# Router logits with the padded weights as loaded operand in four column groups, and token places by 5 products in place of 14, in a two-layer hybrid trunk

## The reference

```python
logits = (t @ router).astype(F32)          # (512, 1024) @ (1024, 8)
top_v, top_i = lax.top_k(logits, TOP_K)    # TOP_K = 2
gates = jax.nn.softmax(top_v, axis=-1)
order = jnp.argsort(e_flat)                # tokens sorted by expert
counts = jnp.bincount(e_flat, length=N_EXPERTS)
out = swiglu(t[tok], w_gate[e], w_up[e], w_down[e])   # per block of one expert
```

## Time and profile before

| what | value |
|---|---|
| median of 3 runs | 2400.32 us (2399.8 to 2401.42) |
| the profiled execution | 2397.78 us |
| its span, first to last instruction | 2395.7 us |
| mean granted clock of TensorE | 0.980 |
| TensorE busy | 2268.1 us (95%) |
| VectorE, ScalarE, GpSimd busy | 1167.0, 942.6, 119.1 us |
| experts stage, from the first expert weight's issue (1166.33 us) | 1229 us of the span |

### The profile page before, as it was taken

One profiled execution on the slowest core, in us unless ns is written; L12 is line 12 of the kernel. 1 busy time (PEld: TensorE's weight loads), 2 busy tenths in 40 slices (PEclk: granted clock), 3 DMA queues, 4 the chain that ended last, 5 costly groups with the idle time before them and its releaser, 6 DMA issues.

```text
span 2395.7 us, 37781 instructions
## 1 busy us (share of the span) xinstructions
PE 2268.1 (95%) x15401; PEld 1932.3 (81%) x15401; DVE 1167.0 (49%) x1563; ACT 942.6 (39%) x1176; POOL 119.1 (5%) x177
## 2 busy tenths in 40 slices
PE   7988999999999888989899999999999998999995
PEld 6864988888878777649687777877779998999994
DVE  3267533323254678473588888888883000001001
ACT  4247432222242444373367677676772000000001
POOL 6101000000000000000000001010100000000000
PEclk9999999999999999999899999999999999999997
DMA  6320223242222000111699999999998768768663
GB/s 196 111 83 6 87 90 106 88 128 97 93 81 79 2 3 3 37 36 41 232 365 345 376 343 368 355 365 349 370 338 292 258 216 271 257 226 281 229 226 106
DMA packets 262117, 451.16 MB, mean 188 GB/s; under 512 B 8360, under 2 KB 148495, under 8 KB 261855
## 3 DMA queue, kind: packets, MB, share of 16 engines
q1 hardware_dynamic: 257216, 435.73, 52.4%
q0 software_dynamic: 4576, 13.41, 2.3%
q10 hardware_dynamic: 190, 0.05, 0.0%
HBM read 436.63 MB, written 12.52 MB: 187 GB/s over the span
## 4 chain that ended last, share of the span: by engine, by line
PE 86%; DVE 6%; ACT 4%; issue 2%; DMA 1%; ACTq 0%; DVEq 0%; POOLq 0%; SPq 0%; POOL 0%
PE bank L704 83%; PE bank L707 3%; DVE arena L2108 1%; DVE w_low L2108 1%; DVE slot L2108 1%; ACT w_high L2026 1%; ACT arena L1636 0%; ACT arena L1737 0%; ACT arena L1645 0%; DMA xs<-sum_rows_d 0%; DMA vec_rows<-in_b_norm_w_dram 0%; DMA sum_rows_d<-arena,idx_now 0%; ACT arena L1613 0%; ACT w_high L1581 0%; DVE arena L2855 0%
## 5 line engine op out<-in xcount | busy, mean ns | idle before, releaser
L2108 DVE TENSOR_TENSOR w_low<-slot,w_high 128x2048 fp32r<-128x2048 f32 x172 | 393.6, 2292 | 325.1 <-ACT w_high L1581 257.9
L704 PE MATMUL bank<-arena 128*128 128x144 f32 (+6 forms) x2672 | 344.6, 298 | 6.1 <-DVE small L2267 2.5
L704 PEld LDWEIGHTS bank<-arena 128*128 128x128 f32 (+4 forms) x2672 | 311.7, 182 | 21.7 <-issue 10.8
L704 PE MATMUL bank<-arena,slot 128*128 128x144 f32 (+4 forms) x2368 | 312.3, 301 | 10.8 <-issue 5.9
L2108 DVE TENSOR_TENSOR arena<-arena,bank 128x512 f32<-128x512 f32 (+2 forms) x99 | 58.7, 593 | 529.9 <-PE bank L704 529.9
L704 PEld LDWEIGHTS bank<-arena,slot 128*128 128x128 f32 (+2 forms) x2368 | 288.7, 184 | 30.4 <-issue 23.4
L2108 DVE TENSOR_TENSOR w_low<-arena,w_high 128x2048 fp32r<-128x2048 f32 x105 | 240.1, 2290 | 25.9 <-ACT w_high L2026 25.1
L2026 ACT ACTIVATE w_high<-slot 128x2048 fp32r<-128x2048 f32 x108 | 206.3, 1915 | 71.0 <-PE bank L704 39.3
L704 PE MATMUL bank<-w_high,xg_high 128*128 128x512 f32 x560 | 227.3, 406 | 6.3 <-DVE w_low L2108 4.2
L2026 ACT ACTIVATE w_high<-arena 128x2048 fp32r<-128x2048 f32 x105 | 201.2, 1921 | 62.3 <-PE bank L704 62.3
L704 PE MATMUL bank<-h_ffn,w_high 128*128 128x512 f32 (+1 forms) x736 | 222.7, 385 | 0.8 <-DVE w_low L2108 0.8
(11 more groups left out here) (367 smaller groups left out, 3265.5 us busy)
## 6 DMA issues: line engine op xcount, KB each, us to landing
slot<-in_moe_w_up_dram SPq DMA_DIRECT2D x86, 1024.0 KB, 6.5
arena<-in_moe_w_gate_dram SPq DMA_DIRECT2D x78, 1024.0 KB, 6.9
arena<-in_moe_w_down_dram SPq DMA_DIRECT2D x64, 1024.0 KB, 6.6
slot<-in_moe_w_down_dram SPq DMA_DIRECT2D x48, 1024.0 KB, 6.3
slot<-in_moe_w_gate_dram SPq DMA_DIRECT2D x34, 1024.0 KB, 5.2
arena<-in_moe_w_up_dram SPq DMA_DIRECT2D x26, 1024.0 KB, 5.9
slot<-in_e_w_in_dram SPq DMA_DIRECT2D x12, 1024.0 KB, 5.4
slot<-in_ff_w_gate_dram SPq DMA_DIRECT2D x11, 1024.0 KB, 5.1
```

What stands on the lines that cost most here:

```text
L704: return pe.matmul(o, lhsT, rhs, start=start, stop=True, skip_group_check=True)
L2108: return dve.tensor_tensor(o, a, b, op)
```

## The change

The operands of the logit products change places. `w_router` is padded to 32 columns with zeros and becomes the loaded operand, 128 tokens of `hT[3]` are streamed. The eight products of a token tile go to the four groups of 32 output rows in turn (k and k + 4 to the same group), so a bank then holds four partial sums of 8 rows each, by expert and token. VectorE copies this bank to `logit_parts`. One product per tile, with `logit_parts` loaded and the 128x8 matrix `group_sum` streamed, adds the four groups and turns the result back into tokens by experts. `group_sum` is built once by GpSimd from `ident`. The places take one product of 32 columns with `before` for all tiles, and one with `ones` for each of the four tiles, which adds that tile's counts to all later column groups at once.

```diff
--- before.py
+++ after.py
@@ -269,7 +269,8 @@
         vc = sb("vc", [P, 95])
         w_dt = sb("w_dt", [P, KT, HEADS])
         w_dt_high, w_dt_low = sb("w_dt_high", [P, KT, HEADS], F32R), sb("w_dt_low", [P, KT, HEADS], F32R)
-        w_router = sb("w_router", [P, KT, N_EXPERTS])
+        w_router = sb("w_router", [P, KT, 32])
+        group_sum = sb("group_sum", [P, N_EXPERTS])
         lora = sb("lora", [P, 2, C_WIDTH])
         small = sb("small", [P, 256])
         small_i = sb("small_i", [P, 16], I32)
@@ -410,6 +411,7 @@
         assert M0 + 1200 + SLOT <= S0 and len(raw_slots) == RAW
         xg_high, xg_low = rounded("xg_high", arena_at + 4 * S0, KT, P), rounded("xg_low", arena_at + 4 * (S0 + 1024), KT, P)
         hid_tok = region(S0 + 2048, 4 * P)
+        logit_parts = region(S0 + 2048, NT, P)
         hid_high = rounded("hid_high", arena_at + 4 * (S0 + 2560), 2, 2, P)
         hid_low = rounded("hid_low", arena_at + 4 * (S0 + 3072), 2, 2, P)
         h_mix = [rounded(f"h_mix{i}", arena_at + 4 * at, KT, SEQ) for i, at in enumerate((4096, 0))]
@@ -565,7 +567,8 @@
                                pattern=[[-1, P]], channel_multiplier=1).then_inc(sem("ident_ready"), 1)
             for k in range(KT):
                 pool.dma_start(w_dt[:, k, :], e_w_in[0, k * P:(k + 1) * P, DT_COL:DT_COL + HEADS]).then_inc(sem("w_dt_loaded"), 16)
-            pool.dma_start(w_router[:, :, :], moe_router[0].rearrange("(k p) e -> p k e", p=P)).then_inc(sem("router_loaded"), 16)
+            link(pool.memset(w_router[:, :, :], 0.0))
+            pool.dma_start(w_router[:, :, 0:N_EXPERTS], moe_router[0].rearrange("(k p) e -> p k e", p=P)).then_inc(sem("router_loaded"), 16)
             pool.dma_start(small[0:HEADS, 0:1], b_dt_bias[0].rearrange("(h a) -> h a", a=1)).then_inc(sem("small_loaded"), 16)
             pool.dma_start(small[0:HEADS, 1:2], b_a_log[0].rearrange("(h a) -> h a", a=1)).then_inc(sem("small_loaded"), 16)
             for r in range(2):
@@ -588,6 +591,9 @@
             pool.wait_ge(sem("bias_loaded"), 16 * HEADS)
             link(pool.memset(bias_w[CHUNK:P, :, SEQ - CHUNK:], -MASKED))
 
+            link(pool.tensor_tensor(group_sum[:, :], ident[:, 0:N_EXPERTS], ident[:, 32:32 + N_EXPERTS], ALU.add))
+            for g in (2, 3):
+                link(pool.tensor_tensor(group_sum[:, :], group_sum[:, :], ident[:, 32 * g:32 * g + N_EXPERTS], ALU.add))
             link(pool.memset(ones[:, :], 1.0))
             link(pool.memset(before[:, :], 1.0))
             select(before[:, :], ALU.is_gt, 0.0, 0, [[1, P]], -1)
@@ -1363,22 +1369,39 @@
 
             if upto >= 6:
                 pe.wait_ge(sem("router_loaded"), 16)
-                b, former = tile("logit_ready", 1)
+                def logits_by_group(t):
+                    b, former = tile("parts_ready", t + 1)
+                    pe.wait_ge(*former)
+                    for k in range(KT):
+                        if k % 4 == 0:
+                            pe.wait_ge(sem("hT_ready"), 24 + 2 * t + k // 4 + 1)
+                        g = slice(32 * (k % 4), 32 * (k % 4) + 32)
+                        m = mm(b[g, 0:P], w_router[:, k, :], hT[3][:, k, P * t:P * (t + 1)], k < 4)
+                    m.then_inc(sem("parts_full"), 1)
+
+                def logits_by_token(t):
+                    pe.wait_ge(sem("parts_ready"), t + 1)
+                    return mm(logits[:, 8 * t:8 * t + 8], logit_parts[:, t, :], group_sum[:, :], t == 0)
+
+                for t in (0, 1):
+                    logits_by_group(t)
+                logits, former = tile("logit_ready", 1)
                 pe.wait_ge(*former)
-                for t in range(NT):
-                    if t == 2:
-                        turn(3)
-                    pe.wait_ge(sem("hT_ready"), 24 + 2 * t + 2)
-                    for k in range(KT):
-                        m = mm(b[:, 8 * t:8 * t + 8], hT[3][:, k, P * t:P * (t + 1)], w_router[:, k, :], t == 0 and k == 0)
-                m.then_inc(sem("logit_full"), 1)
+                logits_by_token(0)
+                logits_by_group(2)
+                turn(3)
+                for t in (1, 2):
+                    logits_by_token(t)
+                logits_by_group(3)
+                logits_by_token(3).then_inc(sem("logit_full"), 1)
 
                 pe.wait_ge(sem("sel_ready"), 1)
                 b, former = tile("place_ready", 1)
                 pe.wait_ge(*former)
-                for t in range(NT + 1):
-                    for s in range(min(t + 1, NT)):
-                        m = mm(b[:, 8 * t:8 * t + 8], (before if s == t else ones)[:, :], sel[:, s, :], t == 0)
+                mm(b[:, 0:8 * NT], before[:, :], sel.rearrange("p t e -> p (t e)"), True)
+                for s in range(NT):
+                    later = b[:, 8 * s + 8:8 * NT + 8].rearrange("p (t e) -> p t e", e=N_EXPERTS)
+                    m = mm(later, ones[:, :], sel[:, s:s + 1, :].to_broadcast([P, NT - s, N_EXPERTS]), False)
                 m.then_inc(sem("place_full"), 1)
                 pe.wait_ge(sem("place_ready"), 1)
                 for i in range(WARM_UP):
@@ -2627,7 +2650,14 @@
 
 
             if upto >= 6:
+                def logits_taken(t):
+                    dve.wait_ge(sem("parts_full"), t + 1)
+                    dve.tensor_copy(logit_parts[:, t, :], bank["parts_ready", t + 1][:, 0:P]).then_inc(sem("parts_ready"), 1)
+
+                for t in (0, 1, 2):
+                    logits_taken(t)
                 turned(3, 3)
+                logits_taken(3)
                 L, E2 = NT * N_EXPERTS, [P, NT, N_EXPERTS, N_EXPERTS]
                 dve.wait_ge(sem("logit_full"), 1)
                 dve.tensor_copy(logit, bank["logit_ready", 1][:, 0:L].rearrange("p (t e) -> p t e", e=N_EXPERTS)).then_inc(sem("logit_ready"), 1)
```

## The result

The changed kernel takes 2378.25 us, median of 4 runs (2376.1 to 2379.18), beside 2400.06 us (2397.12 to 2401.42, 4 runs) for the kernel before. The ratio is 0.9912, 95% interval 0.9896 to 0.9927. The profiled execution took 2377.97 us, its span 2375.9, 19.8 us less than before.

What follows compares the result with a forecast made beforehand. TensorE, busy 95% of the span, was taken as the bound, with no other work covering these products. Logits 4.35 plus places 3.85 gave 8.2 us off the median 2400.3: 2392.1 us, with an 8-in-10 range of 2389.0 to 2396.5.

Steps and rivals of the forecast that it cites:

- What is hidden: Set-up: GpSimd's memset and three additions, at most 3.6 us, lie under over 40 us of cover; padding adds no transfer.
- Step 1: Logits: tiles 0 and 1 start at 1130.76 as before and end at about 1132.0.
- Step 2: Logits: VectorE is late; its 0.28 us bank copies start after `turned(3, 2)`, costing TensorE 0.3 us wait plus 0.35 us product.
- Steps 3 to 5: Logits: tile 2, `turn(3)`, then tile 3's second half at the low clock; VectorE copies the logits 4.35 us earlier.
- The mark "16 records in 0.5 to 0.6 us": Expected sign in the logits: 128x32 loads in fours, with each token tile's 16 records in that time.
- The mark of 6.5 us to the copy: Expected sign: VectorE copies the logits 6.5 us after the first logit product instead of 11.0.
- The Trainium skill's rule: Logits: loads run under a product only in another row group; 1.0 us a tile, total gain about 7.2 instead of 8.2.
- 1.7 us either way: Gathering `first_rows`: its low-clock stretch may shift, costing or saving 1.7 us, the largest term of the range.
- Two groups at a time: Rival for the logits: only two column groups overlap, eight rounds per tile; gain 7.4, 2392.9 us, chance 8%.
- no overlap at all: Rival for the logits: column groups do not run side by side; gain 1.4, 2398.9 us, chance 6%.
- Records run singly: Rival for the logits: each load and product runs to its end, 0.4 us a record; 2414 us, chance 3%.
- The low clock through all of `first_rows`: Rival for the gathering: 64 records take 15.4 us in place of 9.78; gain 2.6, 2397.7 us, chance 5%.

Runs made afterwards that it cites:

- a1_shift800: Kernel before plus an unused array of 800 bytes per partition behind `w_router`, no instruction changed: 2387.65 us, ratio 0.996.
- a2_after_plus32: Changed kernel plus 32 unused bytes per partition right ahead of the arena: 2389.65 us, ratio 0.9967 to the kernel before.
- a3_arena32: Kernel before plus 32 unused bytes right ahead of the arena alone: 2387.5 us, ratio 0.996.
- b2_logits_only: Changed kernel with the old 14 place products and 32 unused bytes ahead of the arena: 2398.99 us, ratio 1.0008 to the kernel before.
- k1_xg128: Changed kernel with the experts' loaded buffers 128 bytes further within the arena: 2375.07 us, ratio 0.9902 to the kernel before.
- h1_slots64: Changed kernel plus 64 unused bytes ahead of the weight slots, moving slots and arena alike: 2376.41 us, ratio 0.9908.
- h2_both64: Changed kernel plus 64 unused bytes ahead of the weight slots and 64 more ahead of the arena: 2387.0 us, ratio 0.9958.
- h4_both32: Changed kernel plus 32 unused bytes ahead of the weight slots, moving slots and arena alike: 2375.49 us, ratio 0.9907.

## Why the prediction was wrong

The mechanism it priced was right, and its sum was right for the stage. The failed step is in "What is hidden": it takes GpSimd's instructions as the only effect of the set-up ("The padding adds no transfer"), and so puts the new addresses at nothing without a reason. The padding and `group_sum` move every array declared after them by 768 + 32 = 800 bytes. That is worth 10.4 us by `a1_shift800` and 11 to 14 us by `a2_after_plus32`, more than the whole sum. By the rule of distances the 768 bytes, three times 256, change nothing: the 32 bytes of `group_sum` do, and `a3_arena32` has the same gain from 32 bytes alone (0.996).

- **Logits.** 4.35 us forecast, 4.7 measured, within the bounds of 3.5 and 5.2. Step 1 was 1.2 us for tiles 0 and 1 and took 1.08. Step 2, a copy at 0.28 us, was 0.28 to 0.29, and VectorE was the late one. Steps 3 to 5 kept the order given. The mark "16 records in 0.5 to 0.6 us" held for tiles 0 and 1 (1.08 us for 32) and was just missed by tile 2 (0.65). The mark of 6.5 us to the copy came out at 6.3. One small step was off: the second half of tile 3 was to run at the low clock, and the timeline's windows show 1.00 up to 1128.20.

```profile
1122.24:1128.20 5.96, 4.34 (x80) 3.28 (x79) 3.77 (x10) 2.83 (x5) 0.00 (x0) 1.00 0.95 324
1128.90:1139.10 10.20, 6.70 (x17) 4.74 (x18) 7.83 (x26) 0.23 (x1) 0.00 (x0) 0.50 0.61 247
```

- **Places.** 3.85 forecast, 3.84 measured, ten records at the low clock in 2.32 us, as the second of these windows has them (0.50). The wider stream is hidden by the loads as assumed.
- **The Trainium skill's rule** (TensorE: Matmul & The Clock Gate, Part 3: Packing small matmuls), by which loads of all rows wait for the running product, would have made 1.0 us a tile with four groups. The runs do not agree: a tile took 1.84 us in one group, 0.97 in two and 0.54 in four. Each load record lasts at least 106 ns, as the next line has them, so the 32 loads of tiles 0 and 1 are over 3.4 us one after another. They fit into 1.08 us, so the loads of other columns did run under the products.

```profile
L710 PEld LDWEIGHTS bank<-arena,w_router x64: 106/110/110, 1122.2 to 1127.3; 128*32 128x32 f32 x64
```

- **GpSimd.** Its memset took 0.38 us, and its transfer of the weights landed 1100 us before use: nothing on the path.

```profile
L570 POOL MEMSET w_router<- x1: 377/377/377, 6.3 to 6.3; 128x256 f32 x1
```

- **The clock.** "1.7 us either way" for `first_rows`: there it stayed, 9.78 us then and now. Later stretches moved 2.3 us in favour of the changed kernel; in `b2_logits_only` such stretches took back all of the 4.7 us. This term was too narrow, though it did not make the miss.
- **The stage as a whole.** 8.5 us against 8.2. `a2_after_plus32`, the changed kernel at a slow distance, gains 8.4 us in all, but with an interval of 5 to 11 us it is partly luck that this comes so near to 8.2. The experts' first weight was to be asked for at 1158.1; it was 1149.27, 8.5 us of the difference being the upstream shift.

```profile
1149.27 1.08 SPq L212 DMA_DIRECT2D slot<-in_moe_w_gate_dram  x2
```

- **The rivals.** Two groups at a time and no overlap at all are excluded by 1.08 against 1.94 and 3.68 us. Records run singly would have shown 0.4 us each. The low clock through all of `first_rows` would have made it 15.4 us.

What would have caught it: the prediction listed as a mark that the distance from the table of turns to the end might change. It named no mark for the 1130 us ahead of the change, because nothing there was edited.

## What to carry to other kernels

A change of an array's size is also a change of every later address: before an unexpected difference is put down to instructions, add the same number of bytes as an unused array to the old kernel, and pad the new one until its operands lie as far apart as in the old. A few bytes are enough to matter: 32 did it here. When TensorE is busy 100% in both traces, compare how many records fit into an equal window. Small products that use few output columns gain by column groups only up to the engine that reads the results: with two groups the stage won 4.1 us, with four 4.7.

## What the runs showed of the hardware

A float32r product of 512 columns took 228.9 to 229.5 ns when its streamed operand began 64 bytes past its loaded one, counted modulo 256, and 232.3 to 234.3 ns at 32, 96, 128, 160, 192 and 224. At a distance of 0 it took 228.5 to 230.1 ns; that case is in the experts' third buffer alone, where `k1_xg128` moved it to 128 and made it slow. The difference is 2% of every such record, 10 us of this kernel. The distance decides; moving both operands together changed nothing in `h1_slots64`, `h2_both64` and `h4_both32`. What it is in the chip (how the two reads share the memory) no run shows, and distances finer than 32 bytes were not tried.

Four column groups with 128 rows loaded each ran 32 float32 records in 1.08 us, 0.034 us each, as dense as the 64x64 products of the earlier trace rows; two groups took 1.94 us and one took 3.68.
